# Norm sums, token-wise projections and first tiles regrouped in a two-block transformer kernel

## What is computed

```python
# block 1, layer 0: gated short convolution, then the convolutional feed-forward
b, c, h = split(rms_norm(x) @ w_in);  x = x + (b * causal_dwconv(c * h)) @ w_out
x = x + (silu(g) * u) @ w_down        # g, u = split(causal_dwconv(rms_norm(x) @ w_up))
# shared latent keys and values, then layer 1: latent attention, 8 heads of 128 + 64
ckv = rms_norm(x) @ w_dkv;  kv = rms_norm(ckv[:256]) @ w_ukv
q = rms_norm(rms_norm(x) @ w_dq) @ w_uq;  x = x + attention(q, kv) @ w_o
x = x + conv_ffn(rms_norm(x));  x = rms_norm(x)
# block 2: three mixers side by side, shift, scale and gate from a conditioning vector
h = rmsnorm(x) * (1 + scale1) + shift1;  a_u, a_v, b_q, b_k, b_v, c_q, c_k, c_v = split(h @ w_in)
y = [spatial_gating(a_u, a_v), stick_breaking(b_*), dilated_window(rope(c_q), rope(c_k), c_v)]
x = x + (1 + gate1) * (y @ w_out)
x = x + (1 + gate2) * conv_ffn(rmsnorm(x) * (1 + scale2) + shift2);  return rmsnorm(x)
```

## Time and profile before

| | us |
|---|---|
| median of 3 runs | 1821.82 |
| lowest, highest | 1821.19, 1825.4 |
| the profiled execution | 1823.36 |
| its span, first to last instruction | 1821.5 |
| PE busy | 1759.3 |
| DVE, ACT, POOL busy | 1161.5, 700.8, 400.2 |
| mean granted PE clock | 0.986 of full speed |

### The profile page before, as it was taken

One profiled execution on the slowest core, in us unless ns is written; L12 is line 12 of the kernel. 1 busy time (PEld: TensorE's weight loads), 2 busy tenths in 40 slices (PEclk: granted clock), 3 DMA queues, 4 the chain that ended last, 5 costly groups with the idle time before them and its releaser, 6 DMA issues.

```text
span 1821.5 us, 22484 instructions
## 1 busy us (share of the span) xinstructions
PE 1759.3 (97%) x7820; PEld 1413.1 (78%) x7820; DVE 1161.5 (64%) x1509; ACT 700.8 (38%) x975; POOL 400.2 (22%) x172
## 2 busy tenths in 40 slices
PE   7999999999999999999999999899999899999997
PEld 6888788888887765878888888687558688888885
DVE  6566777777557765577777666574766677777223
ACT  4223444443224335344444322332564444444221
POOL 3444100002443320310000255434101300000342
PEclk9999999999999999999999999899999899999998
DMA  4332232324663220232322565222101132322331
GB/s 180 103 105 94 96 98 92 102 94 162 211 206 104 70 70 1 70 104 92 101 95 93 172 213 204 95 93 91 37 1 35 62 101 92 101 95 92 105 104 69
DMA packets 52187, 186.84 MB, mean 103 GB/s; under 512 B 5792, under 2 KB 6048, under 8 KB 52000
## 3 DMA queue, kind: packets, MB, share of 16 engines
q1 hardware_dynamic: 50832, 182.47, 29.7%
q10 hardware_dynamic: 1296, 3.58, 0.5%
HBM read 183.94 MB, written 2.10 MB: 102 GB/s over the span
## 4 chain that ended last, share of the span: by engine, by line
PE 90%; DVE 7%; ACT 2%; issue 1%; DMA 0%; POOL 0%; DVEq 0%; SPq 0%; ACTq 0%
PE ps L1461 27%; PE ps L1463 27%; PE ps L1462 27%; PE ps L1624 1%; PE ps L1719 1%; PE ps L1686 1%; DVE rb L890 1%; DVE RAB L1073 1%; PE ps L1631 1%; DVE stat L1149 1%; PE ps L1707 1%; DVE QXL L897 0%; PE ps L1650 0%; PE ps L1709 0%; PE ps L1726 0%
## 5 line engine op out<-in xcount | busy, mean ns | idle before, releaser
L500 POOL TENSOR_TENSOR WL<-raw,WH 128x1024 fp32r<-128x1024 f32 x159 | 389.2, 2448 | 1375.1 <-ACT WH L549 1375.1
L1461 PE MATMUL ps<-XH,WH 128*128 128x512 f32 x1560 | 614.6, 394 | 18.2 <-DVE XL L897 9.6
L1462 PE MATMUL ps<-XL,WH 128*128 128x512 f32 x1560 | 609.8, 391 | 0.0
L1463 PE MATMUL ps<-XH,WL 128*128 128x512 f32 x1560 | 609.7, 391 | 0.0
L549 ACT ACTIVATE WH<-raw 128x1024 fp32r<-128x1024 f32 x291 | 308.4, 1060 | 580.6 <-PE ps L1463 578.2
L1461 PEld LDWEIGHTS ps<-XH,WH 128*128 128x128 f32 x1560 | 294.4, 189 | 86.9 <-POOL WL L500 9.6
L1462 PEld LDWEIGHTS ps<-XL,WH 128*128 128x128 f32 x1560 | 294.5, 189 | 61.5 <-issue 1.0
L1463 PEld LDWEIGHTS ps<-XH,WL 128*128 128x128 f32 x1560 | 294.4, 189 | 61.6
L1461 PE MATMUL ps<-HH,WH 128*128 128x512 f32 x528 | 205.5, 389 | 0.0
L1462 PE MATMUL ps<-HL,WH 128*128 128x512 f32 x528 | 205.5, 389 | 0.0
L1463 PE MATMUL ps<-HH,WL 128*128 128x512 f32 x528 | 205.4, 389 | 0.0
(11 more groups left out here) (245 smaller groups left out, 1911.5 us busy)
## 6 DMA issues: line engine op xcount, KB each, us to landing
raw<-w_tiles SPq DMA_DIRECT2D x291, 512.0 KB, 3.2
ada<-ada_tiles SPq DMA_DIRECT2D x32, 512.0 KB, 5.4
trig<-ada_tiles SPq DMA_DIRECT2D x16, 512.0 KB, 7.0
out_x<-X SPq DMA_DIRECT2D x8, 256.0 KB, 2.0
X<-x_in SPq DMA_DIRECT2D x2, 512.0 KB, 8.5
X<-x_in ACTq DMA_DIRECT2D x2, 512.0 KB, 8.2
RAB<-c_in SPq DMA_DIRECT2D x2, 512.0 KB, 4.9
MK<-mask_in ACTq DMA_DIRECT2D x1, 1024.0 KB, 5.0
```

Of the source, the lines that this page charges most:

```text
L500: nc.gpsimd.tensor_tensor(WL[k % SPL][:, :], raw[:, k, :], f32(WH[k % SPL][:, :]), ALU.subtract).then_inc(s_lo, 1)
L1461: mm(bank, h, xh, start=first, stop=False)
L1462: mm(bank, h, xl, start=False, stop=False)
L1463: return mm(bank, lo, xh, start=False, stop=last)
```

## The change

It has these parts:

- `sum_squares` of UP0, UP1 and DKV moves into the first tile, behind its chunk 5 (`within`); that of the latent norm moves from behind DQ's tile 0 to behind tile 1.
- For the norms in `APART` (before IN2, before UP2, at the end) `acc` is summed over the tokens without the last chunk, into `ps[5]`, and PE adds the last chunk's squares straight from `SQ` (and `AT`); small DVE operations join the parts (`early_sums`, `whole_sums`).
- `spread` on DVE goes: PE takes the reciprocal itself, broadcast, as weights against the identity, four 128x128 products.
- V in UKV and eight chunks of IN2 are made token by token: slices of 128 tokens of the input are the weights, 512 weight columns the moving side (`token_dot`, `token_group`). 16 of 18 `turn` groups, `take_v` and most copies go; two are left. In IN2 four such tiles fill four banks together.
- The residual loops of the three `APART` norms are unrolled; in the last chunk ACT squares before it converts the next weight tile, and DVE makes the low half of tile 1 of IN2 and UP2, and of the very first tile, for POOL.
- UP2's first two tiles are interleaved (`two_tiles`).
- X is loaded in eight single chunks, four on ACT's queue and four on SP's, those ahead of raw 1.
- PE runs 14 products on zeros (bf16, 128x384) before the first tile.
- At the end ACT multiplies chunks 5 to 7 by the gain, copies a second spread out of `ps[7]`, and POOL multiplies these chunks by it; DVE does five.

```diff
-            for k in range(RAW):
+            load(0)
+            for m in (1, 3, 5, 7):
+                sp.dma_start(X[:, m, :], x_in[:, m, :]).then_inc(s_in[f"x{m}"], 16)
+            for k in range(1, RAW):
                 load(k)
-                if k < 2:
-                    sp.dma_start(X[:, 4 * k:4 * k + 2, :], x_in[:, 4 * k:4 * k + 2, :]).then_inc(s_in[f"x{2 * k}"], 16)
...
+            pool.wait_ge(s_scaled, len(BY_POOL))
+            pool.wait_ge(s_rsb, 1)
+            for m in BY_POOL:
+                nc.gpsimd.tensor_tensor(X[:, m, :], X[:, m, :], rb[:, :], ALU.mult).then_inc(s_fin_pool, 1)
...
+            def early_sums(n):
+
+                at_end = APART.index(n)
+                dve.wait_ge(s_early, 2 + at_end)
+                if n == N_FIN:
+                    ch.link(v.tensor_scalar(nt[:, 6, :], ps[5][:, 0:4], D * EPS, None, ALU.add))
+                    ch.link(v.scalar_tensor_tensor(nt[:, 7, :], nt[:, 6, :], EPS, ps[5][:, 4:8], ALU.mult, ALU.add))
+                else:
+                    ch.link(v.tensor_copy(nt[:, 6, :], ps[5][:, 0:4]))
+
+            def whole_sums(n):
+                dve.wait_ge(s_ssum, n + 2)
+                v.tensor_tensor(nt[:, 0, :], nt[:, 6, :], ps[4][:, 0:4], ALU.add).then_inc(s_ms, 1)
...
+                        if n in APART and m == KD - 1:
+                            early_sums(n)
+                            if then is not None:
+                                low(then, 0)
+                            continue
                         add_square(n, m, k)
...
             def token_inverse(n):
                 dve.wait_ge(s_root, n + 1)
-                ch.link(v.reciprocal(nt[:, 4, :], nt[:, 2, :]))
-                spread(RA, nt[:, 4, :])
+                v.reciprocal(nt[:, 4, :], nt[:, 2, :]).then_inc(s_dg, 1)
...
                     last = dot(ps[M % 4][:, :], t, k, src[0][:, k, :], src[1][:, k, :], k == 0, k == KD - 1)
+                    if within is not None and k == 5:
+                        sum_squares(within)
                 last.then_inc(s_pe, 1)
+
+            def two_tiles(t, M, before):
+
+                tile_ready(t)
+                tile_ready(t + 1)
+                bank_free(M)
+                bank_free(M + 1)
+                for j, k in ((0, 0), (0, 1), (1, 0), (0, 2), (1, 1), (0, 3), (0, 4), (1, 2), (0, 5), (1, 3), (0, 6),
+                             (0, 7), (1, 4), (1, 5), (1, 6), (1, 7)):
+                    if j == 0:
+                        before(k)
+                    last = dot(ps[(M + j) % 4][:, :], t + j, k, XH[:, k, :], XL[:, k, :], k == 0, k == KD - 1)
+                    if k == KD - 1:
+                        last.then_inc(s_pe, 1)
...
-            def spread(count, bank, src):
+            def spread(count, bank, row):
+
                 pe.wait_ge(s_dg, count)
-                mm(bank[:, :], cc("ones"), src[:, :], start=True, stop=True).then_inc(s_bc, 1)
-
+                for n in range(4):
+                    last = mm(bank[:, n * P:(n + 1) * P], nt[:, row, n:n + 1].to_broadcast([P, P]), cc("ident"),
+                              start=True, stop=True)
+                last.then_inc(s_bc, 1)
+
+
+            pe.wait_ge(s_zero, 1)
+            zeros = rbl[:, :].bitcast(BF16)
+            for _ in range(14):
+                mm(ps[7][:, 0:3 * P], zeros[:, 0:P], zeros[:, 0:3 * P], start=True, stop=True)
...
+            def token_group(t0, m0, tiles, width, rows, ready=None):
+
+                per = KD // tiles
+                for tt in range(tiles):
+                    tile_ready(t0 + tt)
+
+                    def step(n, kk):
+                        M, k = m0 + n, per * tt + kk
+                        if k == 0:
+                            bank_free(M)
+                        if n == 0 and ready:
+                            ready(k)
+                        return token_dot(ps[M % 4][:, 0:width], t0 + tt, kk, width, XH[:, k, rows(n)], XL[:, k, rows(n)],
+                                         k == 0, k == KD - 1)
+                    if tt < tiles - 1:
+                        for kk in range(per):
+                            for n in range(4):
+                                last = step(n, kk)
+                        last.then_inc(s_pe, 1)
+                    else:
+                        for n in range(4):
+                            for kk in range(per):
+                                last = step(n, kk)
+                            last.then_inc(s_pe, 1)
...
-                if k == 0:
+                if k == 1:
                     sum_squares(N_LK)
```

More of the change, by code:

```diff
@@ L88 @@
     ("UP1", 2 * FF, [1]), ("DN1", 24, [0, 0, 1]),
[L89 removed]
+    ("IN2", 8, [0, 0, 0, 4]), ("IN2R", 2, [1]), ("IN2F", 12, [1]), ("OUT2", 8, [1]), ("UP2", 2 * FF, [1]), ("DN2", 24, [0, 0, 1]),
 )
@@ L109, in halves @@
 def halves(t0):
-    own = set()
+    own = {0}
     for name in ("UP0", "UP1", "UP2"):
         own |= set(range(t0[name] + SPL, t0[name] + SPL + 2 * FF))
+    own |= {t0["IN2"] + 1, t0["UP2"] + 1}
     return own
@@ L348, in build @@
         SQ0 = [sum(NORM_CHUNKS[:i]) for i in range(10)]
+        APART = (N_FIN, N_F2, N_END)
+        ACC0 = [sum(NORM_CHUNKS[:i]) - sum(n < i for n in APART) for i in range(10)]
         E_A, E_F0, E_KV, E_Q, E_F1, E_M2, E_F2 = range(7)
@@ L599, in body @@
                                 .then_inc(s_sq2, 1)
-                repeat(act, KD // 4, body, peel=KD // 4 if phase == PHASES[-1][0] else 0)
+                        if late:
+                            ahead(T0[phase] + (k + 1) * tiles_per_m - 1, i, per)
+                repeat(act, KD // 4, body, peel=KD // 4 if n in APART else 0)
             def up(f, phase, bias):
@@ L1173, in _ @@
             dve.wait_ge(s_cact, 2)
-            residual("DN1", 3, None, None, N_FIN, modulation=1, second=True)
+            residual("DN1", 3, None, None, N_FIN, modulation=1, second=True, then=T0["IN2"] + 1)
             dve.wait_ge(s_ada, 6 * KD)
@@ L1426, in _ @@
             class_lo(3)
-            residual("OUT2", 1, None, None, N_F2, gate=2)
+            residual("OUT2", 1, None, None, N_F2, gate=2, then=T0["UP2"] + 1)
+            whole_sums(N_F2)
             token_inverse(N_F2)
@@ L1463, in dot, with wide @@
                 return mm(bank, lo, xh, start=False, stop=last)
-            def wide(t, M, i=0, per=0, before=None, src=(XH, XL), ready=True):
+            def wide(t, M, i=0, per=0, before=None, src=(XH, XL), ready=True, within=None):
                 if ready:
@@ L1501, in a_ch @@
                 for k in range(4):
-                    wide(T0["A_CH"] + k, M0["A_CH"] + k, i, 4, inputs(E_A) if start and k == 0 else None)
+                    if start:
+                        tile_ready(T0["A_CH"] + k)
+                    else:
+                        tile_ready(T0["A_CH"] + 4 + k, i - 1, 4)
+                    wide(T0["A_CH"] + k, M0["A_CH"] + k, i, 4, inputs(E_A) if start and k == 0 else None, ready=False)
                     if start and k == 2:
@@ L1530, in body @@
                             tile_ready(T0[phase] + 4 + k, i - 1, 4)
-                        wide(T0[phase] + k, M0[phase] + k, i, 4, inputs(e) if start and k == 0 else None, ready=False)
-                        if start and k == 0 and n is not None:
-                            sum_squares(n)
+                        if start and n is None and k < 2:
+                            if k == 0:
+                                two_tiles(T0[phase], M0[phase], inputs(e))
+                            continue
+                        wide(T0[phase] + k, M0[phase] + k, i, 4, inputs(e) if start and k == 0 else None, ready=False,
+                             within=n if start and k == 0 else None)
                 repeat(pe, FF // 2, body, peel=1)
@@ L1565, in turn, with token_dot @@
                 for n in range(4):
-                    src = AT[:, aux % 2, n::4] if strided else AT[:, aux % 2, n * P:(n + 1) * P]
-                    last = nc.tensor.transpose(ps[5 + aux % 2][:, n * P:(n + 1) * P], src, cc("ident"))
+                    last = nc.tensor.transpose(ps[5 + aux % 2][:, n * P:(n + 1) * P], AT[:, aux % 2, n::4], cc("ident"))
                 last.then_inc(s_aux, 1)
+            def token_dot(bank, t, blk, width, xh, xl, first, last):
+                h = WH[t % SPL][:, blk * width:(blk + 1) * width]
+                lo = WL[t % SPL][:, blk * width:(blk + 1) * width]
+                mm(bank, xh, h, start=first, stop=False)
+                mm(bank, xl, h, start=False, stop=False)
+                return mm(bank, xh, lo, start=False, stop=last)
@@ L1570, in _ @@
             for k in range(3):
-                wide(T0["DKV"] + k, M0["DKV"] + k, before=inputs(E_KV) if k == 0 else None)
-                if k == 0:
-                    sum_squares(N_KV)
+                wide(T0["DKV"] + k, M0["DKV"] + k, before=inputs(E_KV) if k == 0 else None,
+                     within=N_KV if k == 0 else None)
             for k in range(KQ):
```

(7 more changed lines are left out.)

243 lines of the change are left out of this document (129 added, 114 removed).

## The result

| | before | after |
|---|---|---|
| time, median of four runs | 1822.34 us (1821.19 to 1825.4) | 1811.66 us (1811.45 to 1812.03) |
| profiled execution, its span | 1823.36, 1821.5 | 1811.55, 1809.7 |
| PE busy | 1759.3 | 1755.6 |

The ratio after/before is 0.9933, with a 95% interval of 0.992 to 0.9945: faster by 10.7 us. The forecast was 1805.8, a gain of 16.0; 1811.66 lies in the range of 1799 to 1813.5. The profiled executions stand 11.8 us apart, and that is what I break down here.

The account below looks back on a forecast made before the run. PE, busy 1759.3 of 1821.5 us, was taken as the bound except at seven places. Terms -2.3 + 0.9 + 2.5 + 2.4 + 2.7 + 3.9 + 2.9 + 1.8 + 1.2 = 16.0 us gave 1805.8, range 1799 to 1813.5.

Parts of the forecast that it names:

- the seven places: Where PE's spacing leaves 0.227 us: first tile, joints before UP0, DKV, UP1, IN2, UP2, and the tail.
- rival (d): UKV and IN2: token-wise products don't keep 0.227 us, so gain is lost or the kernel is slower; chance 0.03.
- 1, the start: First tile: XH[4] queues behind raw 1's conversion and PE idles before chunk 4; -2.3 us (0 to -4).
- 3, DKV to UQ: DKV's early sum delays UKV's start by 1.75, but dropped V transpositions and spread wait gain; +2.5 us (0 to 4.5).
- UKV near 600.4: UKV's first product expected near 600.4 us, less what was saved ahead, from DKV's delay of 1.75.
- 4 and 6, the joints: Before IN2 and UP2: shorter chains, +2.4 and +2.9 us; faster first tiles, +2.7 and +1.8.
- my two cases: UP2's first two tiles, interleaved: 12.05 us with a full clock, 13.3 with 3 us of half rate.
- 5, the transpositions: IN2: ten tiles with a transposition become two, each costing 0.49 us; +3.9 us (3.6 to 4.2).
- 7, the tail: Behind the last product: shorter chain and split final chunks, POOL ending last; +1.2 us (-0.3 to 2).
- the better of my two cases: Tail with the spread at 1.12 us, net +1.8; the other case has 2.08, net -0.1.
- rival (b): Early queues lose more: the start costs 4 us and DKV's stage gives 0; 1810 us, chance 0.2.
- rival (c): First tiles of IN2 and UP2: streams don't gain, PE waits for POOL's WL at half rate; 1810.3 us, chance 0.12.

Follow-up runs that it names:

- kv_sum_back: The changed kernel with DKV's sum of squares behind its first tile again, as before the change; median 1811.11 us, ratio 0.9937.
- no_zero: The changed kernel without the 14 products on zeros; median 1812.42 us, ratio 0.9947.
- old_loads: The changed kernel with paired X loads and the early raw 1 back, zero products and DVE's low half kept; median 1807.87 us, ratio 0.9918.
- up_sum_back: The changed kernel with the sums of squares of UP0 and UP1 behind their first tiles again; median 1813.01 us, ratio 0.9945.
- best: The changed kernel with old load order, DKV's root before the weight conversion, earlier angle steps in IN2 and two final chunks on POOL; median 1800.66 us, ratio 0.9872.
- angle_early: The changed kernel with ACT's and DVE's angle steps of IN2 two and three tiles earlier; median 1809.9 us, ratio 0.9933.

## Why the prediction came out as it did

**What bounds the kernel** held: what changed the time were PE's waits and its extra work at the seven places, and besides them only the clock in the windowed part; PE is 97% busy in both. The new products by token kept 0.227 us (tile by tile 5.44 in IN2), so rival (d) fell. The sign and the main terms were right; the gain was 10.7 for 16.0. The steps that were off:

**1, the start: -3.7 for -2.3.** The mechanism is the one told: ACT at raw 1, XH[4] behind it, POOL's WL beside XL, PE idle 3.3. Its times were nearly right: raw 1 converted at 13.26 (12.7 forecast), the last XL step done at 19.28 (19.0). With the 1.8 of the full clock that makes 2.1. The term was sized too small by the clock: half rate came back after the wait and stayed until 20.07 (1.5 us), and I had named 1.7 as "up to" and put only 0.5 of it into the sum. This is one draw: in kv_sum_back, after a wait of 2.26, no half rate followed and the start lost 2.2; in the nine profiles with this start the loss lies between 2.2 and 4.8. The Trainium skill ("TensorE: Matmul & The Clock Gate", Part 1) says that the unit slows when idle and only sustained work frees it. The traces agree in part: with the zero products as without them (no_zero) the first tile has a stretch at half rate, but kv_sum_back kept full rate behind its wait.

**3, DKV to UQ: +1.65 for +2.5.** UKV's start came 1.3 late for 1.75 (kv_sum_back: 1.34). From there to the attention 2.96 of the 4.26 came: PE waits 0.39 for a rope bank and some 0.8 more at UQ's start, and half rate in UKV cost 2.08 for 1.73. "UKV near 600.4" became 603.27: 600.4 and the 3.7 lost at the start, less 0.4 from UP0 and less 0.5, as the delay was smaller than 1.75.

**4 and 6, the joints: right.** Chains +2.6 and +2.7 (2.4 and 2.9), streams +3.1 and +1.4 (2.7 and 1.8). In IN2 the clock stayed full and the wait for WL was 0.48, not 0.8 (in old_loads, up_sum_back and best IN2's first tile lost 2.1 to 2.4 instead, at half rate); in UP2 the two tiles took 13.74, for 12.05 and 13.3 in my two cases.

**5, the transpositions: +2.5 for +3.9.** The price was right (0.44 to 0.49). What I missed is what is late next. Without the groups PE reaches group 2's banks earlier, and DVE's copies of them stand behind the angle steps, two of which take 2.5 for 0.43 beside POOL. angle_early shows that the order is the cause: the wait goes.

**Not in the forecast: -1.5 in the windowed part**, at half rate, in code that nobody touched.

**7, the tail: +2.0 for +1.2.** The chain gave 2.07, the split 0. I had "POOL ends last": it does among the engines (1807.19, which is 9.97 behind the X update), but the outputs' transfer ends at the same time with or without it, which no term of mine held. The spread ran at the high clock, so the better of my two cases came; by its own figures that case is 3.45 + 1.12 + 0.9 + 0.7 + 3.84 = 10.0 for 12.06, a gain of 2.05 and not the 1.8 that I wrote. This is luck by 0.9: where the last spread was slower, in four of the 13 profiles, the chain took 5.11 to 5.76 for 4.63.

Against the sum: -1.4 (start), -0.85 (stage 3), -1.4 (copies), -1.5 (windows), +0.6 (IN2's joint), -0.6 (UP2), +0.8 (tail) are -4.1 with the small rest, which makes 11.9 of 16.0 in the profile. The range held with little to spare, and the clock's share in this goes both ways: 1.5 lost in the windowed part and 1.0 more at the start than I had priced, 0.9 gained in the last spread. The rest of the way to 10.7 lies between profiles and medians: the profiled run of before stands 1.0 above its median, that of after 0.1 below. Of rival (b) the start came (3.7 for 4), its stage 3 at nothing didn't; rival (c), with 1810.3 the nearest in time, was wrong in its mechanism: both streams gained.

## What to carry to other kernels

An instruction that waits for the last load of a queue must not stand ahead of work that is ready: moving one conversion behind the chunks brought the first sum 3.8 us forward (1.9 in the median), and one root ahead of a conversion was worth 4.9 in DKV, more than most parts of the change. When a step is freed, look at once at who empties its banks and what is queued ahead of that copy. And before a final loop is shared among engines, compare it with the time its outputs need to leave.
